# Moving one 256-column tile home, dropping its own product order, and adding one full fp32 product per FFN stage

## The reference

```
m = c_act @ w + b                       # shift, scale, gate from the condition
h = rmsnorm(x, g) * (1.0 + scale) + shift
swiglu:   (silu(h @ w_gate) * (h @ w_up)) @ w_down        # 1024 -> 2816 -> 1024
conv_ffn: (silu(conv(h @ w_up)[gate]) * conv(h @ w_up)[val]) @ w_down
```

## Time and profile before

| | |
|---|---|
| timed runs, median | 1774.44 us |
| profiled execution, its own time | 1783.76 us |
| its span on the core | 1782.0 us |
| PE busy | 1742.4 us, 98% |
| PE weight loads busy | 1699.3 us, 95% |
| DVE busy | 1452.5 us, 82% |
| ACT busy | 956.5 us, 54% |
| DMA | 426.23 MB, mean 239 GB/s |

### The profile page before, as it was taken

One profiled execution on the slowest core, in us unless ns is written; L12 is line 12 of the kernel. 1 busy time (PEld: TensorE's weight loads), 2 busy tenths in 40 slices (PEclk: granted clock), 3 DMA queues, 4 the chain that ended last, 5 costly groups with the idle time before them and its releaser, 6 DMA issues.

```text
span 1782.0 us, 34261 instructions
## 1 busy us (share of the span) xinstructions
PE 1742.4 (98%) x14686; PEld 1699.3 (95%) x14686; DVE 1452.5 (82%) x1750; ACT 956.5 (54%) x1254; POOL 0.2 (0%) x4
## 2 busy tenths in 40 slices
PE   5999999999999999999999999999999999999999
PEld 4999999998999999999999999999999998989999
DVE  7799899988898879897558989765899888567776
ACT  4444566676533454445765333566655556675553
POOL 0000000000000000000000000000000000000000
PEclk9999999999999999999999999999999999999999
DMA  9999734443798859895436988343387545316550
GB/s 395 411 420 332 308 143 166 166 144 141 313 394 328 331 204 389 326 379 183 149 141 227 387 309 352 147 154 124 127 302 282 210 147 187 141 72 218 186 199 34
DMA packets 68149, 426.23 MB, mean 239 GB/s; under 512 B 7488, under 2 KB 10832, under 8 KB 31824
## 3 DMA queue, kind: packets, MB, share of 16 engines
q1 hardware_dynamic: 63936, 416.22, 61.3%
q10 hardware_dynamic: 4112, 8.62, 1.4%
HBM read 423.74 MB, written 3.17 MB: 240 GB/s over the span
## 4 chain that ended last, share of the span: by engine, by line
PE 93%; DVE 3%; ACT 3%; DMA 1%; issue 0%; DVEq 0%; SPq 0%; ACTq 0%
PE bank L1575 25%; PE bank L1576 24%; PE bank L1577 24%; PE bank L1632 2%; PE bank L1634 2%; PE bank L1633 2%; PE bank L1588 1%; PE bank L1688 1%; PE bank L1602 1%; PE bank L1991 1%; DMA mix<-mods 1%; PE bank L1591 1%; ACT w_hi L496 1%; PE bank L1859 1%; ACT work L719 0%; PE bank L1972 0%
## 5 line engine op out<-in xcount | busy, mean ns | idle before, releaser
L1575 PE MATMUL bank<-h_hi,w_hi 128*128 128x256 f32 x2504 | 696.2, 278 | 0.0
L1577 PE MATMUL bank<-h_hi,w_lo 128*128 128x256 f32 x2504 | 695.2, 278 | 0.0
L1576 PE MATMUL bank<-h_lo_rest,w_hi 128*128 128x256 f32 x2504 | 695.2, 278 | 0.0
L915 DVE TENSOR_TENSOR w_lo<-raw,w_hi 128x2048 fp32r<-128x2048 f32 x267 | 609.5, 2284 | 91.4 <-ACT w_hi L496 90.4
L496 ACT ACTIVATE w_hi<-raw 128x2048 fp32r<-128x2048 f32 x276 | 527.9, 1913 | 159.7 <-PE bank L1577 146.1
L1575 PEld LDWEIGHTS bank<-h_hi,w_hi 128*128 128x128 f32 x2504 | 473.0, 189 | 0.0
L1576 PEld LDWEIGHTS bank<-h_lo_rest,w_hi 128*128 128x128 f32 x2504 | 470.2, 188 | 0.0
L1577 PEld LDWEIGHTS bank<-h_hi,w_lo 128*128 128x128 f32 x2504 | 470.1, 188 | 0.0
L1575 PE MATMUL bank<-a_hi,w_hi 128*128 128x256 f32 x1280 | 358.6, 280 | 0.8 <-DVE a_lo L1293 0.8
L1577 PE MATMUL bank<-a_hi,w_lo 128*128 128x256 f32 x1280 | 355.4, 278 | 0.0
L1576 PE MATMUL bank<-a_lo,w_hi 128*128 128x256 f32 x1280 | 355.4, 278 | 0.0
(11 more groups left out here) (304 smaller groups left out, 1986.3 us busy)
## 6 DMA issues: line engine op xcount, KB each, us to landing
raw<-weights SPq DMA_DIRECT2D x276, 1024.0 KB, 5.3
modws<-mods SPq DMA_DIRECT2D x144, 768.0 KB, 6.7
mix<-mods SPq DMA_DIRECT2D x5, 1024.0 KB, 8.8
mix<-mods ACTq DMA_DIRECT2D x8, 512.0 KB, 13.3
biases<-scratch ACTq DMA_DIRECT2D x1, 2048.0 KB, 13.3
mix<-biases ACTq DMA_DIRECT2D x4, 512.0 KB, 3.8
modws<-mods SPq DMA_DIRECT2D x1, 1024.0 KB, 11.6
x<-xin SPq DMA_DIRECT2D x1, 1024.0 KB, 10.9
```

The lines of the kernel that those rows point to most:

```text
L915: eng.tensor_tensor(w_lo[g % NW][:, :], raw[g % NRAW][:, :], w_hi[g % NW][:, :], ALU.subtract).then_inc(sems["wlo"], 1)
L1575: eng.matmul(dst, ah, bh, start=start, stop=False, skip_group_check=skip)
L1576: eng.matmul(dst, ah, bl, start=False, stop=False, skip_group_check=skip)
L1577: return eng.matmul(dst, al, bh, start=False, stop=stop, skip_group_check=skip)
```

## The change

Two edits. First, tile 0 of the low part gets no home and no order of its own: all eight low tiles lie in one tensor `h_lo_all`, in order, and `three()` is used for tile 0 as for the others. The 16 columns of the gap go to `gap2` behind it, so that every tensor behind keeps its address. Second, each FFN stage does one fp32 product of ones by ones, 128 columns, into bank 6, between its second block and its third. Nothing reads its result.

```
         h_hi = sb("h_hi", [P, KT, T], F32R)
-        h_lo_rest = sb("h_lo_rest", [P, KT - 1, T], F32R)
-        gap = sb("gap", [P, 16])
-        h_lo_first = sb("h_lo_first", [P, T], F32R)
-        gap2 = sb("gap2", [P, 48])
+        h_lo_all = sb("h_lo_all", [P, KT, T], F32R)
+        gap2 = sb("gap2", [P, 64])
 
         def h_lo(kk):
 
-            return h_lo_rest[:, kk - 1, :] if kk else h_lo_first[:, :]
+            return h_lo_all[:, kk, :]
...
-        z_hi, z_lo = h_hi[:, 1:3, :], h_lo_rest[:, 0:2, :]
+        z_hi, z_lo = h_hi[:, 1:3, :], h_lo_all[:, 1:3, :]
...
-                            if tokens and kk == 0:
-                                eng.matmul(d, h_lo(kk)[:, part], hi[:, kk, :], start=True, stop=False)
-                                eng.matmul(d, h_hi[:, kk, part], hi[:, kk, :], start=False, stop=False)
-                                eng.matmul(d, h_hi[:, kk, part], lo[:, kk, :], start=False, stop=False)
-                            elif tokens:
+                            if tokens:
                                 mm = three(d, h_hi[:, kk, part], h_lo(kk)[:, part], hi[:, kk, :], lo[:, kk, :],
                                            kk == 0, kk == KT - 1)
-                            elif kk == 0:
-                                eng.matmul(d, hi[:, kk, part], h_lo(kk), start=True, stop=False)
-                                eng.matmul(d, hi[:, kk, part], h_hi[:, kk, :], start=False, stop=False)
-                                eng.matmul(d, lo[:, kk, part], h_hi[:, kk, :], start=False, stop=False)
                             else:
...
+            def full_product():
+
+                eng.matmul(bank[6][:, 0:P], con_("ones"), con_("ones"), start=True, stop=True)
+
...
                 gate(0, 0, 0, True)
                 up(0, 0, 1, True)
+                full_product()
                 gate(1, 3, -1)
```

## The result

The change made the kernel slower: 1781.47 us in the median of 13 runs (1775.14 to 1793.42), against 1773.76 us for 13 runs of the kernel before on the same chip; ratio 1.0045, 95% interval 1.0028 to 1.0062 (estimated from all runs, so here and below a ratio need not be the quotient of two medians). The forecast was 1759 us with a range of 1753 to 1776: wrong in sign, and outside the range.

A forecast was written before the change was run, and what follows sets the result against it. PE's own pace, fast or slow, was taken to bound the kernel. Terms 1.5 - 12.4 - 3.4 - 1.0 - 0.3 + 0 = -15.6 us, off the 1774.4 us median, gave 1758.8, say 1759 us; range 1753 to 1776.

The forecast's parts named there:

- What bounds the kernel: Whole kernel: PE, busy 98% of the span, sets the end, with a fast pace of 113.3 ns and a slow 117.8 ns.
- the address does nothing: Rival: the pace belongs to the stage, tile address is without effect, only the six products remain: +1.5 us, 1776 us; chance 0.04.
- Stages 2 and 5 ... -12.4 us: FFN stages 2 and 5, 1392 matmuls each behind the product: slow pace becomes fast, -6.2 us twice.
- The 128-column product leaves PE at the fast pace: Product ahead of each FFN stage's third block: expected to leave 113.3 ns, as at seven mamba places, all fast.
- With no odd tile left nothing should shift the pace within the stage: Stages 2 and 5 behind the product: the fast pace holds, as no wait of PE stands there; supports -12.4 us.
- its price in the openings: Openings with tile 0 at the fast pace cost 27 ns each; stages 3, 7 and 9, 42 each: -3.4 us.
- can bring it back: Stage 0 behind its stop: an opening with tile 0, 64 bytes off, can return slow PE to the fast pace.
- Stage 0: Openings -1.0 us; behind the DVE wait near 73.6 us, -0.3 us if PE restarts fast (6 in 10), +4.9 if slow.
- The product's cost: One product of ones in each of six FFN stages, 0.26 us each: +1.5 us (1.3 to 1.6).
- The mixers: 79 blocks of 48 matmuls between fp32 products: no net change, 0, within -5 to +5 us.
- the one on the slow side: Rival: the product leaves PE slow for 29 blocks of FFN stages; 1776 to 1795 us; chance 0.15.
- 2 and 5 fast need three or more of the others slow: Slow-side rival's threshold: with stages 2 and 5 fast, three or more other stages must be slow to come near zero.

The follow-up runs named there:

- aligned home: Kernels with all eight low tiles of h in one tensor `h_lo_all`, where the kernel before has tile 0 64 bytes off; alone, in plain order, without product: ratio 1.0078.

## Why the prediction was wrong

- *What bounds the kernel*: right. PE's pace, two of them, 113.3 and 117.8 ns, and nearly all of the difference between kernels is in them. The Trainium skill, "TensorE: Matmul & The Clock Gate", section "Step-by-step: what each phase is for", says that loading the next weights doesn't steal read bandwidth from the running matmul. The prediction held the two paces against it. That goes too far: 1319 and 1370 of the same matmuls in the same 155 us, at the same clock, show that the rate has two levels, and no run here shows whether a weight load has to do with it. The rival that was drawn from it, that the address does nothing, is refuted by the 36 of 36 first blocks against 0 of 108.
- *"Stages 2 and 5 ... -12.4 us"*: **the step that failed first.** The size per stage was nearly right (5.5 us in stage 2; forecast 6.2), the base was not. In the profiled execution two stages went at the slow pace, in the median that I subtracted from none. The sign was in front of me: the profiled execution was 9.3 us above the median, and two slow stages at about 5 us make 10. I wrote the 9.3 us down and carried them over as a constant. Without this term the sum is -3.2 us: 1771 us, still faster.
- *"The 128-column product leaves PE at the fast pace", seven of seven*: **the step that failed second.** It is true in mamba and says nothing on this, for all seven come out of the same pace. The windows of the kernel before ahead of the product and behind it (the earlier trace rows has the second):

```profile
260.20:264.80 4.60, 4.60 (x41) 1.00 0.63 228
267.20:271.80 4.60, 4.60 (x43) 1.00 0.29 84
```

  41 in 4.60 us is slow. Seven times slow to fast is what a swap does too. I noted that the product at 624.46 "came out of a slow stage and left it fast", and that the one behind stage 7, a fast stage, left slow; put side by side these were the swap. The one behind stage 3 went from fast to fast, as it did in every profile where stage 3 was fast.
- *"With no odd tile left nothing should shift the pace within the stage"*: right, and so was its price in the openings (stages 3, 7 and 9 shorter by 0.9, 0.6 and 0.8 us, with 0.24 us of product in them). But the odd tile also acted ahead of the third block, where the forecast looked at nothing: with it 19 of 24 stages had a fast second block, without it 24 of 72, and the sum had no term for losing that. **This is the third step that failed.** The reason is the change of pace in the first block, in 36 of 36, together with the wait for DVE behind it. In the kernel with both edits one fault half cancels the other: most stages arrive slow, and the product swaps them to fast. Where the first edit is alone this costs 14 us (0.0078 of 1778.7), and where the second is alone 23 us.
- *An odd tile that "can bring it back"*: half right. It also does the reverse, in 23 of the 36 first blocks; the rows of stage 2 above were in the trace that the prediction was made from.
- *Stage 0*: wrong. It is the one stage that arrives fast with the aligned home (10 of 12), so the product makes it slow: 202.4 us against 196.1 without the product. The wait for `w_lo` at 73.6 us, of which I had expected 0.4 us, is gone, since a slow stage never catches up with DVE.
- *The product's cost* +1.5: right (six times 0.24). *The mixers* 0: right (+0.3 in all).
- *Rivals*: what happened is the one on the slow side with another mechanism: not a state that the product leaves, but a swap. I gave it 0.15. For "2 and 5 fast need three or more of the others slow" the base was wrong too.

The times then add up. The lowest times of aligned kernels, 1769.6 and 1770.1 us, belong by their size to no stage at the slow pace (an estimate, as no profile of them was taken). The changed kernel's 13 times stand at 1775 to 1777 (3), 1780 to 1782 (6), 1786 to 1789 (2) and 1792 to 1793 (2). That is one, two, three and four stages at the slow pace, at 5.7 us each, 2.2 on average. From the arrivals, over all 12 profiles with the aligned home: a swap would leave stage 0 slow in 10 of 12 and each other stage in 14 of 60, and 5 x 14/60 + 10/12 = 2.0. How many stages a single time stands for is worked out from it, not seen; only the profiles show stages.

## What to carry to other kernels

Before a gain is subtracted from a median, ask whether the profiled execution is one of those in the median; when it lies off by a multiple of the very term that is to be removed, it is not. When an instruction seems to leave a state behind, tabulate the state ahead of it as well: seven cases from one incoming state are one case. And where a kernel's pace has two levels that hold for long, one run of a variant, or one median of three, tells little; compare the stages of several profiles. One letter for a whole block can also hide a change inside it: the odd tile seemed only to mend until the steps on both sides of its first read were laid side by side.

## What the runs showed of the hardware

- With the clock at full rate throughout, a stream of 256-column F32R matmuls with a weight load each runs at 113.3 or at 117.8 ns from start to start, and holds either for over 1300 matmuls, with DMA share anywhere from 0.01 to 1.0.
- An odd number of extra products between two blocks, fp32 or F32R, of 32, 64 or 128 columns, changed one pace into the other in 40 of 40 cases; two or four kept it in 12 of 12. A single fp32 product of 96 columns did it in 48 of 48 behind stages 2, 5 and 7, and not behind stage 3, where PE always left it fast. Something in PE or its weight loads may go by turns; what it is no run shows.
- Two products in a row that read 256 columns from an address 64 bytes off a whole tile changed the pace in 36 of 36 first blocks, 23 of them to slow; at the aligned address the same two changed it in 0 of 108. Such reads one at a time, inside a later block, never ended the fast pace (9 of 9 stages with added reads kept it) and at times ended the slow pace: in 5 of 9 stages with added reads, and in stage 0 behind its stop in 2 of 2. An added read of 256 columns from an aligned address inside a block was not tried, so for the added ones the address is not separated from the place.
- A wait of PE's weight loads for DVE of some 0.05 to 0.12 us, where a first block had caught up with the tiles of h, left the pace fast in 22 of 37 stages and slow in 15: 14 of the 24 that were fast ahead of it came out fast, and 8 of the 13 that were slow. In the FFN stages 2 to 9, where that wait did not occur, the pace never changed between the two blocks (43 of 43). What decides behind a wait no run shows; that is where chance comes in.
